# The last gathers, additions and stores of a mixture-of-experts kernel: issued and ordered differently at the program's end

## The reference, cut to what matters

```
def block(args):                       # 128 tokens at a time
    xt, it, gt = args                  # tokens, expert numbers, gates
    ue = u[it]
    ve = v[it]
    a = gelu(einsum('nd,ned->ne', xt, ue))
    return einsum('ne,ned->nd', a * gt, ve)

x = x + peer_ffn(h2, ...)
return x * rsqrt(mean(x * x) + 1e-6) * final_norm_g
```

## Time and profile before

| what | value |
|---|---|
| median of 3 runs | 1759.25 us (1757.31 to 1762.73) |
| the profiled execution's own time | 1762.95 us |
| its span | 1761.2 us |
| busy PE, DVE, ACT, POOL | 96%, 64%, 44%, 49% |
| granted TensorE clock, mean | 0.989 |
| q0 (gathers), q1 (plain transfers): packets' share of 16 engines | 19.9%, 46.1% |
| chain that ended last: PE, POOL, DMA, DVE | 46%, 1%, 1%, 0% |

### The profile page before, as it was taken

One profiled execution on the slowest core, in us unless ns is written; L12 is line 12 of the kernel. 1 busy time (PEld: TensorE's weight loads), 2 busy tenths in 40 slices (PEclk: granted clock), 3 DMA queues, 4 the chain that ended last, 5 costly groups with the idle time before them and its releaser, 6 DMA issues. The chain is left out here.

```text
span 1761.2 us, 30619 instructions
## 1 busy us (share of the span) xinstructions
PE 1694.2 (96%) x10448; PEld 1368.7 (78%) x10448; DVE 1130.5 (64%) x2441; ACT 772.1 (44%) x1258; POOL 861.9 (49%) x713
## 2 busy tenths in 40 slices
PE   6989889999999989999989999999999999999997
PEld 5867645489999989999987777777777777777774
DVE  2675755528888867888546665665656666665665
ACT  5444445444333444555444434434443443444443
POOL 2363340056878780000027665665566665565663
PEclk9999999999999999999999999999999999999999
DMA  5321150054454454776788999999999999999996
GB/s 182 117 74 48 49 192 1 1 203 159 167 171 159 146 186 157 261 256 241 263 288 319 369 337 331 346 342 332 340 349 331 338 358 326 340 354 334 335 351 242
DMA packets 170627, 426.87 MB, mean 242 GB/s; under 512 B 24240, under 2 KB 75568, under 8 KB 170416
## 3 DMA queue, kind: packets, MB, share of 16 engines
q1 hardware_dynamic: 119584, 272.87, 46.1%
q0 software_dynamic: 45056, 134.38, 19.9%
q10 hardware_dynamic: 5904, 18.56, 2.7%
HBM read 389.69 MB, written 36.04 MB: 242 GB/s over the span
## 5 line engine op out<-in xcount | busy, mean ns | idle before, releaser
L2127 PE MATMUL psum<-h2hi,u_hi 128*128 128x512 f32 x1016 | 365.2, 398 | 0.0
L1944 POOL DMA_INDIRECT rows<-in_peer_v,row_i x248 | 245.3, 989 | 215.7 <-PE psum L2161 149.9
L1923 POOL DMA_INDIRECT spot<-acts_first,spot_i x256 | 275.6, 1076 | 84.5 <-issue 78.6
L2128 PE MATMUL psum<-h2hi,u_lo 128*128 128x256 f32 x1024 | 287.0, 280 | 0.0
L2127 PEld LDWEIGHTS psum<-h2hi,u_hi 128*128 128x128 f32 x1016 | 190.7, 188 | 69.5 <-issue 24.3
L1972 ACT ACTIVATE gel<-pre 128x256 f32<-128x256 f32 x128 | 53.5, 418 | 404.0 <-DVE pre L2017 404.0
L2139 PE MATMUL psum<-v_hi,w_hi 128*128 128x512 f32 x512 | 202.6, 396 | 2.3 <-DVE w_lo L2030 2.3
L2007 DVE TENSOR_TENSOR u_lo<-u_raw,u_hi 128x1024 fp32r<-128x1024 f32 x126 | 154.5, 1226 | 76.8 <-ACT u_hi L1962 76.3
L2139 PE MATMUL psum<-v_hi,w_lo 128*128 128x512 f32 x512 | 202.6, 396 | 0.0
L2139 PE MATMUL psum<-v_lo,w_hi 128*128 128x512 f32 x512 | 202.5, 396 | 0.0
L2128 PEld LDWEIGHTS psum<-h2hi,u_lo 128*128 128x128 f32 x1024 | 193.8, 189 | 4.4
(11 more groups left out here) (283 smaller groups left out, 4103.0 us busy)
## 6 DMA issues: line engine op xcount, KB each, us to landing
u_raw<-in_peer_u SPq DMA_DIRECT2D x256, 512.0 KB, 4.6
v_raw<-in_peer_v SPq DMA_DIRECT2D x128, 512.0 KB, 6.9
acts_first<-gel SPq DMA_DIRECT2D x128, 128.0 KB, 2.5
gates<-chunk ACTq DMA_DIRECT2D x32, 512.0 KB, 2.7
g_in<-gates SPq DMA_DIRECT2D x64, 256.0 KB, 7.9
wring<-in_w_in SPq DMA_DIRECT2D x24, 512.0 KB, 3.5
wq_raw<-in_w_query SPq DMA_DIRECT2D x16, 512.0 KB, 5.7
w_out<-in_w_out SPq DMA_DIRECT2D x1, 4096.0 KB, 14.1
```

Of the source, the lines that this page charges most:

```text
L1923: pool.indirect_dma_start(spot[:, t:t + 1], None, spots, bass.IndirectOffsetOnAxis(ap=spot_i[:, t:t + 1], axis=0)).then_inc(s_spot, 16)
L1944: pool.indirect_dma_start(rows[:, slot, :], None, values, bass.IndirectOffsetOnAxis(ap=row_i[:, t:t + 1], axis=0)).then_inc(s_rows[q % PER ...
L2127: pe.matmul(bank, u_hi[:, s % 2, k, :], h2hi[:, k, :], start=(k == 0), stop=False)
L2128: last = pe.matmul(bank[:, 0:DENSE], u_lo[:, s % 2, k, :], h2hi[:, k, GATHERED:T], start=False, stop=(k == KD - 1))
```

## The change

Three things are written otherwise. On POOL, the first two of the four gathers of quad 62 are issued before the rows of quads 60 and 61, each with its own wait for the slot's subtraction. On DVE, the scaling of tile 0 stands behind the last coefficients, the additions of tile 2 ahead of the window of quad 62, those of tile 3 ahead of the window of quad 63, and the scalings of tiles 2 and 3 ahead of the additions of tile 1. And tile 1 is squared by halves: the sum of the first half goes through a small DVE operation (`part` = first sum / 1024 + eps) and enters the root as its bias; its two halves are stored one by one, each when it is scaled.

```diff
--- before.py
+++ after.py
@@ -1819,6 +1819,8 @@
         ss = sb("ss4", [P, NT])
         std = sb("std4", [P, NT])
         rstd = sb("rstd4", [P, NT])
+        ss_half = sb("ss_half", [P, 2])
+        part = sb("ss_part", [P, 1])
 
         s_u = [sem(f"u5_in{i}") for i in range(E)]
         s_v = [sem(f"v_in{i}") for i in range(E)]
@@ -1834,6 +1836,7 @@
                                                                sem("spot_in"), sem("coef_r"), sem("window_r"))
         s_acc, s_fg, s_sq, s_std, s_rstd, s_fin, s_store = (sem("acc_r"), sem("fgain_in"), sem("sumsq4"), sem("std4_r"),
                                                             sem("rstd4_r"), sem("final_r"), sem("stored"))
+        s_part = sem("ss_part_r")
         s_again = keep["u_again"]
         block = ctx.enter_context(nc.Block())
 
@@ -1899,10 +1902,14 @@
             load_v(2, 2)
             over_rounds(sp, loads)
             sp.dma_start(fgain[:], dram["final_norm_g"].to_broadcast([P, D])).then_inc(s_fg, 16)
-            for i, t in enumerate(ORDER):
+            for i, t in enumerate(ORDER[:-1]):
                 sp.wait_ge(s_fin, 2 * i + 2)
                 sp.dma_start(columns_of(dram["out"], t), x_sb[:, t, :]).then_inc(s_store, 16)
-            sp.wait_ge(s_store, 16 * NT)
+            for half in range(2):
+                c = slice(half * BANK, (half + 1) * BANK)
+                sp.wait_ge(s_fin, 2 * NT - 1 + half)
+                sp.dma_start(columns_of(dram["out"][:, c], ORDER[-1]), x_sb[:, ORDER[-1], c]).then_inc(s_store, 16)
+            sp.wait_ge(s_store, 16 * (NT + 1))
 
         def token(q, j):
             return q // 32 * P + j * 32 + q % 32
@@ -1923,18 +1930,22 @@
                         pool.indirect_dma_start(spot[:, t:t + 1], None, spots,
                                                 bass.IndirectOffsetOnAxis(ap=spot_i[:, t:t + 1], axis=0)).then_inc(s_spot, 16)
 
+            def gather_last(z, js):
+                for j in js:
+                    if z:
+                        pool.wait_ge(s_vlo, NKEYS - E + j + 1)
+                    else:
+                        pool.wait_ge(s_ulo, NKEYS - E + j - 1)
+                    t = token(QUADS - PER + z, j)
+                    pool.indirect_dma_start(last_rows[z][:, j, :], None, values,
+                                            bass.IndirectOffsetOnAxis(ap=row_i[:, t:t + 1], axis=0)).then_inc(s_last[z], 16)
+
             def gather_rows(r):
+                if r == ROUNDS - 2:
+                    gather_last(0, (0, 1))
                 if r == ROUNDS - 1:
-
-                    for z in range(PER):
-                        for j in range(4):
-                            if z:
-                                pool.wait_ge(s_vlo, NKEYS - E + j + 1)
-                            elif j == 0:
-                                pool.wait_ge(s_ulo, NKEYS - 2)
-                            t = token(QUADS - PER + z, j)
-                            pool.indirect_dma_start(last_rows[z][:, j, :], None, values,
-                                                    bass.IndirectOffsetOnAxis(ap=row_i[:, t:t + 1], axis=0)).then_inc(s_last[z], 16)
+                    gather_last(0, (2, 3))
+                    gather_last(1, range(4))
                     return
                 for q in range(r * PER, (r + 1) * PER):
                     for j in range(4):
@@ -1991,13 +2002,21 @@
             gelu(0, 0)
             split_w(0, 0)
             over_rounds(act, body)
-            for i, t in enumerate(ORDER):
+            for i, t in enumerate(ORDER[:-1]):
                 act.wait_ge(s_acc, 2 * i + 2)
                 act.activation(junk[:], x_sb[:, t, :], ACT.Square, accum_out=ss[:, i:i + 1]).then_inc(s_sq, 1)
                 act.wait_ge(s_sq, i + 1)
                 if i == 0:
                     act.wait_ge(s_rstd, 1)
                 act.activation(std[:, i:i + 1], ss[:, i:i + 1], ACT.Sqrt, bias=eps[:, 0:1], scale=1.0 / D).then_inc(s_std, 1)
+            i, t = NT - 1, ORDER[-1]
+            for half in range(2):
+                c = slice(half * BANK, (half + 1) * BANK)
+                act.wait_ge(s_acc, 2 * i + 1 + half)
+                act.activation(junk[:, c], x_sb[:, t, c], ACT.Square, accum_out=ss_half[:, half:half + 1]).then_inc(s_sq, 1)
+            act.wait_ge(s_sq, NT + 1)
+            act.wait_ge(s_part, 1)
+            act.activation(std[:, i:i + 1], ss_half[:, 1:2], ACT.Sqrt, bias=part[:, 0:1], scale=1.0 / D).then_inc(s_std, 1)
 
         @block.vector
         def _(dve):
@@ -2071,6 +2090,18 @@
                         weigh(n, s, turn)
                         rest_w(n, s)
 
+            def final(i):
+
+                if i == 0:
+                    dve.wait_ge(s_fg, 16)
+                dve.wait_ge(s_std, i + 1)
+                dve.reciprocal(rstd[:, i:i + 1], std[:, i:i + 1]).then_inc(s_rstd, 1)
+                dve.wait_ge(s_rstd, i + 2)
+                for half in range(2):
+                    c = slice(half * BANK, (half + 1) * BANK)
+                    dve.scalar_tensor_tensor(x_sb[:, ORDER[i], c], x_sb[:, ORDER[i], c], rstd[:, i:i + 1], fgain[:, c],
+                                             ALU.mult, ALU.mult).then_inc(s_fin, 1)
+
             dve.memset(eps[:], EPS).then_inc(s_rstd, 1)
             dve.wait_ge(s_picked, 16)
 
@@ -2091,24 +2122,20 @@
             dve.wait_ge(s_coef, 1)
             over_rounds(dve, body)
             coefficients(ROUNDS, 1)
+            final(0)
             for z in range(PER):
+                dve.wait_ge(s_out, NKEYS)
+                for half in range(2):
+                    accumulate(2 + z, half, 2 * z + half)
                 weights_of(ROUNDS, z, 1)
-            dve.wait_ge(s_out, NKEYS)
-            for m in range(SPOTS):
-                accumulate(2 + m // 2, m % 2, m)
-            dve.wait_ge(s_fg, 16)
-            for i, t in enumerate(ORDER):
-                if i == 1:
-                    dve.wait_ge(s_quad, QUADS)
-                    for half in range(2):
-                        accumulate(1, half, SUMS + half)
-                dve.wait_ge(s_std, i + 1)
-                dve.reciprocal(rstd[:, i:i + 1], std[:, i:i + 1]).then_inc(s_rstd, 1)
-                dve.wait_ge(s_rstd, i + 2)
-                for half in range(2):
-                    c = slice(half * BANK, (half + 1) * BANK)
-                    dve.scalar_tensor_tensor(x_sb[:, t, c], x_sb[:, t, c], rstd[:, i:i + 1], fgain[:, c],
-                                             ALU.mult, ALU.mult).then_inc(s_fin, 1)
+            final(1)
+            final(2)
+            dve.wait_ge(s_quad, QUADS)
+            for half in range(2):
+                accumulate(1, half, SUMS + half)
+            dve.wait_ge(s_sq, NT)
+            dve.scalar_tensor_tensor(part[:], ss_half[:, 0:1], 1.0 / D, eps[:, 0:1], ALU.mult, ALU.add).then_inc(s_part, 1)
+            final(3)
 
         @block.tensor
         def _(pe):
```

## The result

The changed kernel takes 1758.55 us (median of 22 runs, 1755.99 to 1761.35), the kernel before 1762.14 in as many runs beside it: a ratio of 0.9981, interval 0.9973 to 0.9989, or 3.4 us less (1.9 to 4.8). That is a gain, and less than the 0.3% called measurable in the prediction; with 22 runs the interval became narrower than that. The forecast was 3.85 us less, a ratio of 0.9978. The forecast median of 1755.4 started from three runs of before with a median of 1759.25; over 22 runs before is 1762.14, 2.9 higher. So the measured 1758.55 lies 3.2 over the forecast median and only just inside the range, which ended at 1758.8.

The account below looks back on a forecast made before the run. The end was taken as bound by the last gathers, TensorE's last quad, then VectorE's serial additions and scalings and the last store. 1.20 + 1.75 + 0.9 = 3.85 us less, median 1755.4, range 1753.0 to 1758.8.

Parts of the forecast that it names:

- TensorE's hole, 1.20: TensorE idle before quad 63, waiting for the last gather; closing it by two gathers issued ahead saves 1.20 us.
- the gathers' 2.49: GpSimd's last gather issued 2 x 1.245 = 2.49 us sooner with two gathers ahead; only 1.20 was expected to count.
- The rival of the collision: Tile 0's store delays the last gathers' landing, by at most its whole 4.0; time 1758.0; chance 0.08.
- Order and halves of the square, 1.75: First addition of tile 1 to last scaling takes 4.11 instead of 5.86 us, saving 1.75 (bounds 0.9 and 2.1).
- The margin of the scalings: On VectorE, scalings of tiles 2 and 3 end 0.28 us before tile 1's additions can begin.
- The rival of the slipped scaling: One or both VectorE scalings don't fit under the last quads: time 1756.6 or 1758.2; chance 0.12.
- The last store, 0.9: Tile 1's store in halves shortens last scaling to landing from 4.0 to 3.1 us, saving 0.9 (bounds 0 and 1.5).
- part 4: Section on storing the last tile in halves, saving 0.9 us; stores of tiles 0, 2 and 3 leave VectorE's path.
- The row-gather wait that would have made it slower: On GpSimd, the two early gathers wait late and hold up eight row gathers; 1764 if for tile 127; chance 0.04.
- A gain over 5.3: Whole kernel faster by more than the 0.3%, 5.3 us, that a measurement can tell from no change; chance 0.20.

Follow-up runs that it names:

- gathers only: Kernel before with only the two gathers issued ahead, old VectorE order, whole square and store: quads 60/61 start to span end 18.09 us, against 18.82 before.
- order only: Kernel before with only VectorE's new order; gathers last, whole square, whole store: quads 60/61 start to span end 17.20 us, against 18.82 before.
- none ahead: Changed kernel with no gather issued ahead of the rows: quads 60/61 start to span end 16.08 us, against 14.52 for the changed kernel.
- the store of tile 0 held: Changed kernel without gathers ahead, tile 0's store also waiting until tile 2 is scaled: quads 60/61 start to span end 15.76 us.
- gathers and order: Kernel before with two gathers ahead and VectorE's new order, whole square and store: quads 60/61 start to span end 15.69 us, against 18.82 before.
- late wait: Changed kernel with all gathers of quad 62, the two ahead too, waiting for the subtraction of u tile 127: 1.0042 of before (1.0027 to 1.0057).

## Why the prediction was right, and where its terms were off

*TensorE's hole, 1.20.* Right in size: 1.22. Its ground was right too: one gather ahead closes it as well as two, so of the gathers' 2.49 only the hole counts. What the prediction did not say is that this term isn't there alone. Without the new order VectorE arrives 0.6 late and half of it is lost (gathers only: additions 0.61 sooner, tail 0.73 shorter). Without the gathers the hole was 0.24 and 0.33 wider than before (order only, none ahead) and 0.06 wider with the store of tile 0 held. So on top of the rest of the change the gathers are worth 16.08 - 14.52 = 1.56 by these two profiles. The rival of the collision did not happen in the changed kernel, where the last gather was in 1.7 early. Where the gathers were late, up to 0.3 may be its price, and not the 4.0 of its upper bound; since that landing scatters by more, it is not shown.

*Order and halves of the square, 1.75.* Measured 5.86 - 4.03 = 1.83: 1.41 from the order, 0.42 from the halves. The square of 512 columns took 0.63 and 0.61, the interpolated value. The margin of the scalings was forecast as 0.28 and is 0.16. The starts are where they were forecast, within 0.1; but I had counted the second scaling as 1.52, which is the step from start to start, and its end comes 0.09 after that, and the additions begin 0.03 sooner than in the sum. The rival of the slipped scaling was that close. By the drain of the Trainium skill (ScalarE: Activation LUTs, What ACT_TABLE_LOAD costs) the root would come about 1.38 after the load. The trace of the changed kernel does not show it either: the root starts as soon as the load ends (1743.74 after 1742.44 + 1.28).

*The last store, 0.9.* This is the term that was mis-sized: 4.59 - 3.35 = 1.24. Halving is 0.74 to 0.81 of it, a little under my 0.9. By the figures of the Trainium skill (DMA: Bandwidth & Descriptors, Anatomy of one DMA) an estimate gives 0.6 for halving; the page has them from transfers issued by GpSimd, and these stores are SyncE's. The measured 0.74 to 0.81 is over that: halves landed in 2.9, a whole tile with nothing moving in front of it in 3.7. The other 0.4 to 0.5 belongs to the order: 4.59 and 4.47 with the old order, 4.13, 4.10 and 4.08 with the new one. It is a queue of stores. In the old order the last three follow 1.52 apart, and the last one is issued while the ones before it are still moving; in the new order they are long gone. The traces show it on stores of one size: from issue to landing the last one took 4.1 in before and in gathers only, and 3.7 in order only, in gathers and order, and with the whole store and halved square. The two stretches below hold its issue, at 1756.6 in before and at 1751.6 in gathers and order; the last two columns are the busy share of the DMA engines and GB/s:

```profile
1756.50:1757.00 0.50, 0.00 (x0) 0.00 (x0) 0.11 (x1) 0.00 (x0) 0.00 (x0) 0.50 0.95 336
```
```profile
1751.50:1752.00 0.50, 0.00 (x0) 0.00 (x0) 0.10 (x1) 0.00 (x0) 0.00 (x0) 0.50 0.00 0
```

I had named the earlier stores in part 4 and given them no price; my 4.0 was the median of four stores, of which the last had waited.

*Sum.* 1.22 + 1.83 + 1.24 = 4.29 in the two profiles, 3.4 (1.9 to 4.8) in time; the forecast was 3.85. The interval in time holds both, so it does not say which of the two sums is nearer. That the median came out inside the range of 1753.0 to 1758.8 is in part luck: the three runs it started from were 2.9 under the 22, and 0.25 more would have put it outside. The row-gather wait that would have made it slower held up what was said when it was made late, but cost 6.6 from the last spot gather on and not 4.7; in the changed kernel it cost nothing. A gain over 5.3 did not come.

## What to carry to other kernels

At the end of a program, count what each engine still has in its queue when the last data arrive, and move out of the way all that doesn't need them; only then is an earlier arrival worth its time. Price the two together: here they gave 0.73 and 1.62 alone and 3.13 together, because without the new order half of the earlier arrival was lost, and because in the run with the order alone the last gather came 0.24 later. And measure such a change from a landmark just ahead of it: the steps repeat to 0.01 us where whole executions scatter by 5. Check with an earlier mark that the landmark itself has not moved; in the late wait it had, by 2.2.

## What was not expected of the hardware

The part of the program in front of the edits, the same in all runs, makes nearly all of the scatter of the times: its first spot gather came 908.2 to 914.5 us after the start, the landmark 829.5 to 832.1 later (833.4 with the late wait), and the last 28.11 to 28.13 of that did not scatter at all. A 512 KB store issued while gathers were still moving landed in 6.2 and 6.3 instead of 3.9. The last gather of the program took 6.4 to 7.8 to land when issued at the same place behind the same gathers (-3.62 to -3.64), while the engines' steps repeated to 0.01. And VectorE's scaling of 512 columns by one value per partition took 0.49, where the same scaling with a second tensor takes 0.75.
